# Gated linear attention: the next head's gate inside the first unit, and the backward chunk states on GpSimd beside the forward ones on VectorE

## The reference

```python
def gla_chunked(q, k, v, log_a):            # chunks of C = 64 tokens, N = 16 chunks
    b = jnp.cumsum(gc, axis=-2)             # within a chunk
    ref = b[..., C // 2 - 1:C // 2, :]
    q_in, k_in = qc * jnp.exp(b - ref), kc * jnp.exp(ref - b)
    A = jnp.where(mask, jnp.einsum('nbhid,nbhjd->nbhij', q_in, k_in), 0.0)
    o_intra = jnp.einsum('nbhij,nbhjv->nbhiv', A, vc)
    b_last = b[..., -1:, :]
    q_inter, k_state = qc * jnp.exp(b), kc * jnp.exp(b_last - b)
    decay = jnp.exp(b_last[..., 0, :])
    def step(state, inp):
        qi, ki, vi, di = inp
        o = jnp.einsum('bhid,bhdv->bhiv', qi, state)
        state = state * di[..., None] + jnp.einsum('bhjd,bhjv->bhdv', ki, vi)
        return state, o

def gla_branch(...):
    la_f = jax.nn.log_sigmoid(lr_f @ w_g_f + b_g_f) / GLA_TAU     # and la_b
    o_b = flip(gla_chunked(flip(q), flip(k), flip(v), flip(la_b)))
    o = rmsnorm(o_f + o_b, out_norm)
```

## Time and profile before

| | |
|---|---|
| median of 3 runs | 2673.72 us (2667.28 to 4069.49) |
| the profiled execution | 2673.68 us |
| its span | 2671.9 us |
| busy: TensorE, VectorE, ScalarE, GpSimd | 89%, 48%, 38%, 17% |
| mean granted TensorE clock | 0.949 |

### The profile page before, as it was taken

How to read it: one execution, slowest core, us unless ns; L and a number is a source line. 1 busy time by engine, 2 the same in 40 slices (tenths; PEclk the granted TensorE clock), 3 DMA queues, 4 the chain that set the end, 5 groups by cost and what they waited for, 6 DMA issues and landing times. The chain is left out here.

```text
span 2671.9 us, 31271 instructions
## 1 busy us (share of the span) xinstructions
PE 2373.3 (89%) x11010; PEld 1768.2 (66%) x11010; DVE 1279.2 (48%) x2042; ACT 1023.0 (38%) x1655; POOL 451.1 (17%) x502
## 2 busy tenths in 40 slices
PE   7999677986999994988899997997988899998997
PEld 4877355762444442767677886886776777886885
DVE  4288676323111115455615775354455615775354
ACT  5221366222111114555443444144555543444233
POOL 1058143113222213211111000002211111000000
PEclk9999798897999996999999999998999999999998
DMA  6200300133999887101111003012101110003012
GB/s 193 83 32 1 126 1 1 10 96 112 323 350 341 304 269 281 40 25 32 30 37 28 11 32 127 32 48 94 40 25 32 32 42 20 11 32 127 32 49 86
DMA packets 213549, 239.46 MB, mean 90 GB/s; under 512 B 50849, under 2 KB 170913, under 8 KB 213409
## 3 DMA queue, kind: packets, MB, share of 16 engines
q1 hardware_dynamic: 202928, 220.80, 25.3%
q0 software_dynamic: 9440, 16.83, 1.7%
q10 hardware_dynamic: 1040, 0.00, 0.0%
HBM read 211.80 MB, written 41.52 MB: 95 GB/s over the span
## 5 line engine op out<-in xcount | busy, mean ns | idle before, releaser
L106 PE MATMUL ps<-WT_lo,HT_hi 128*128 128x512 f32 x832 | 327.4, 394 | 0.0
L107 PE MATMUL ps<-HT_hi,WF_lo 128*128 128x512 f32 (+1 forms) x800 | 314.1, 393 | 0.0
L105 PE MATMUL ps<-HT_hi,WU_hi 128*128 128x512 f32 (+1 forms) x704 | 289.5, 411 | 16.6 <-DVE H_lo L2131 13.2
L106 PE MATMUL ps<-H_lo,WU_hi 128*128 128x512 f32 (+1 forms) x704 | 277.4, 394 | 0.0
L1570 PE MATMUL ps<-WT,MIX 128*128 128x512 f32 x496 | 225.0, 597 | 2.9 <-DVE MIX L2089 2.9
L105 PE MATMUL ps<-W_hi,HT_hi 128*128 128x512 f32 x512 | 204.6, 400 | 8.8 <-DVE MIX_lo L2272 5.9
L952 POOL TENSOR_TENSOR WF_lo<-WF,WU_hi 128x1024 fp32r<-128x1024 f32 (+1 forms) x44 | 112.2, 2551 | 567.3 <-ACT WU_hi L1162 567.3
L107 PE MATMUL ps<-W_hi,MIX_lo 128*128 128x512 f32 x512 | 201.8, 394 | 0.0
L106 PEld LDWEIGHTS ps<-WT_lo,HT_hi 128*128 128x128 f32 x832 | 158.9, 191 | 31.9
L107 PEld LDWEIGHTS ps<-HT_hi,WF_lo 128*128 128x128 f32 (+1 forms) x800 | 151.1, 189 | 33.8
L105 PEld LDWEIGHTS ps<-HT_hi,WU_hi 128*128 128x128 f32 (+1 forms) x704 | 133.9, 190 | 56.1 <-DVE H_lo L2131 14.0
(11 more groups left out here) (420 smaller groups left out, 5072.7 us busy)
## 6 DMA issues: line engine op xcount, KB each, us to landing
WT<-in_w_gate SPq DMA_DIRECT2D x31, 1024.0 KB, 5.7
WT<-in_w_up SPq DMA_DIRECT2D x31, 1024.0 KB, 9.2
MIX<-in_w_down SPq DMA_DIRECT2D x31, 1024.0 KB, 8.5
WF<-in_w_in SPq DMA_DIRECT2D x48, 512.0 KB, 3.9
WT<-in_w_out SPq DMA_DIRECT2D x6, 2048.0 KB, 8.1
H<-in_x SPq DMA_DIRECT2D x16, 512.0 KB, 8.1
h_dram<-H SPq DMA_DIRECT2D x16, 512.0 KB, 3.0
H<-h_dram SPq DMA_DIRECT2D x16, 512.0 KB, 11.9
```

Of the source, the lines that this page charges most:

```text
L105: pe.matmul(o, lh, rh, start=(i == 0), stop=False)
L106: pe.matmul(o, lh, rl, start=False, stop=False)
L107: mm = pe.matmul(o, ll, rh, start=False, stop=(i == last))
```

## The change

The gate of head h + 1 is computed earlier. On TensorE `gates(h + 1)` moves between the two halves of head h's first unit and writes banks 6 and 7 (free once `ks_copy(h)` is done), on ScalarE `gate(h + 1)` stands behind the first half's evacuation of that unit, ahead of the second half's, and on VectorE `gate(h + 1)` stands ahead of `scan_states(h)`. The backward states go to GpSimd: `scan_back(h)`, 15 steps of a multiplication and an addition, each waiting for the one before. `gt` = cum - middle goes from VectorE to GpSimd too (`from_middle`). ScalarE's `exps` takes `la` first and then waits for GpSimd's `gt`. `outputs(h)` waits for the backward states as well.

```diff
-            GLA_STEPS[g_pe] += [("a", h), ("kt", h), ("kv", h)] + [("z", h + 1)] * more + [("o", h), ("ms", h)]
+            GLA_STEPS[g_pe] += [("a", h), ("kt", h)] + [("z", h + 1)] * more + [("kv", h), ("o", h), ("ms", h)]
...
+            GLA_STEPS[g_pool] += [("stb", h)] + [("gt", h + 1)] * more
...
-                for u in range(2, 16):
+                def from_middle(h):
+                    pool.wait_ge(*gla(L, "c", h))
+                    settle(pool, settled)
+                    pool.tensor_tensor(gt.rearrange("p (c i) -> p c i", c=NCH), cc, refs.unsqueeze(2).to_broadcast([P, NCH, CH]), ALU.subtract).then_inc(g_pool, 1)
+
+                def scan_back(h):
+                    pool.wait_ge(*gla(L, "kvc", h))
+                    pool.wait_ge(ul_ready, L * NU + 7 + 3 * h)
+                    if h == 0:
+                        settle(pool, settled)
+                        hc.link(pool.memset(st[64:P, NCH - 1, :], 0.0))
+                    for c in range(NCH - 2, -1, -1):
+                        settle(pool, settled)
+                        hc.link(pool.tensor_scalar(st[64:P, c, :], st[64:P, c + 1, :], decay[64:P, c + 1:c + 2], None, ALU.mult))
+                        settle(pool, settled)
+                        o = pool.tensor_tensor(st[64:P, c, :], st[64:P, c, :], kv[64:P, c + 1, :], ALU.add)
+                        if c > 0:
+                            hc.link(o)
+                    o.then_inc(g_pool, 1)
+                    pool.wait_ge(*gla(L, "stb", h))
+                for u in range(2, 5):
                     unit_lo(u)
+                from_middle(0)
+                unit_lo(5)
+                for h in range(4):
+                    unit_lo(6 + 3 * h)
+                    if h < 3:
+                        scan_back(h)
+                        unit_lo(7 + 3 * h)
+                        from_middle(h + 1)
+                        unit_lo(8 + 3 * h)
+                scan_back(3)
...
                 def exps(h):
                     act.wait_ge(*gla(L, "d", h))
+                    act.activation(la, la, ACT.Exp, scale=1 / 16.0)
+                    act.wait_ge(*gla(L, "gt", h))
...
-                    evac(*under[h][0])
+                    evac(*under[h][0], between=(lambda: gate(h + 1)) if h < 3 else None)
                     kv_copy(h)
-                    if h < 3:
-                        gate(h + 1)
                     evac(*under[h][1])
...
-                        mm = pe.matmul(bank(2 + half), wgs[:, h, :], lrz[:, half * HALF:(half + 1) * HALF], start=True, stop=True)
+                        mm = pe.matmul(bank(6 + half), wgs[:, h, :], lrz[:, half * HALF:(half + 1) * HALF], start=True, stop=True)
...
                 def outputs(h):
                     pe.wait_ge(*gla(L, "st", h))
+                    pe.wait_ge(*gla(L, "stb", h))
+                    if h < 3:
+                        pe.wait_ge(*gla(L, "t", h + 1))
...
-                    dve.tensor_tensor(chunks(gt), cc, refs.unsqueeze(2).to_broadcast([P, NCH, CH]), ALU.subtract)
+                    dve.sem_inc(g_dve, 1)
...
-                        dve.scalar_tensor_tensor(out=st[0:64, c, :], in0=st[0:64, c - 1, :], scalar=decay[0:64, c - 1:c], in1=kv[0:64, c - 1, :], op0=ALU.mult, op1=ALU.add)
-                        o = dve.scalar_tensor_tensor(out=st[64:P, b, :], in0=st[64:P, b + 1, :], scalar=decay[64:P, b + 1:b + 2], in1=kv[64:P, b + 1, :], op0=ALU.mult, op1=ALU.add)
+                        o = dve.scalar_tensor_tensor(out=st[0:64, c, :], in0=st[0:64, c - 1, :], scalar=decay[0:64, c - 1:c], in1=kv[0:64, c - 1, :], op0=ALU.mult, op1=ALU.add)
...
                 for h in range(4):
                     causal(h)
+                    if h < 3:
+                        gate(h + 1)
                     scan_states(h)
                     if h < 3:
-                        gate(h + 1)
                         products(h + 1)
                     finish(h)
```

More of the change, by code:

```diff
@@ L397, in program @@
         u_w, u_ready, u_evac = sems("u_w", 2), sem("u_ready"), sems("u_evac", 2)
-        g_pe, g_act, g_dve = sem("g_pe"), sem("g_act"), sem("g_dve")
-        GLA_STEPS = {g_pe: [("z", 0)], g_act: [("t", 0), ("e", 0)], g_dve: [("d", 0), ("k", 0), ("q", 0)]}
+        g_pe, g_act, g_dve, g_pool = sem("g_pe"), sem("g_act"), sem("g_dve"), sem("g_pool")
+        GLA_STEPS = {g_pe: [("z", 0)], g_act: [("t", 0), ("e", 0)], g_dve: [("c", 0), ("d", 0), ("k", 0), ("q", 0)], g_pool: [("gt", 0)]}
         for h in range(4):
             more = h < 3
-            GLA_STEPS[g_pe] += [("a", h), ("kt", h), ("kv", h)] + [("z", h + 1)] * more + [("o", h), ("ms", h)]
-            GLA_STEPS[g_act] += [("ks", h), ("kvc", h)] + [("t", h + 1), ("e", h + 1)] * more + [("sq", h), ("r", h)]
-            GLA_STEPS[g_dve] += [("am", h), ("st", h)] + [("d", h + 1), ("k", h + 1), ("q", h + 1)] * more + [("done", h)]
+            GLA_STEPS[g_pe] += [("a", h), ("kt", h)] + [("z", h + 1)] * more + [("kv", h), ("o", h), ("ms", h)]
+            GLA_STEPS[g_act] += [("ks", h)] + [("t", h + 1)] * more + [("kvc", h)] + [("e", h + 1)] * more + [("sq", h), ("r", h)]
+            GLA_STEPS[g_dve] += [("am", h)] + [("c", h + 1), ("d", h + 1)] * more + [("st", h)] + [("k", h + 1), ("q", h + 1)] * more + [("done", h)]
+            GLA_STEPS[g_pool] += [("stb", h)] + [("gt", h + 1)] * more
         GLA_AT = {step: (s, i) for s, steps in GLA_STEPS.items() for i, step in enumerate(steps)}
@@ L942, in layer @@
             def layer(L):
-                hc = Chain(pool, pool_chain, L * 2 * NT + base)
+                hc = Chain(pool, pool_chain, L * (2 * NT + 117) + base)
                 pool.wait_ge(h_in, L * NT + NT)
@@ L981, in layer @@
                 nt_pool(pool, hc, L * 2 + 4)
-                assert hc.n == 2 * NT
+                assert hc.n == 2 * NT + 117
             layers(pool, layer)
@@ L1220, in gate @@
                         hs, bias = slice(half * HALF, (half + 1) * HALF), vl[:, L_GB + h:L_GB + h + 1]
-                        act.activation(la[:, hs], bank(2 + half), ACT.Identity, bias=bias)
-                        o = act.activation(gt[:, hs], bank(2 + half), ACT.Abs, bias=bias)
+                        act.activation(la[:, hs], bank(6 + half), ACT.Identity, bias=bias)
+                        o = act.activation(gt[:, hs], bank(6 + half), ACT.Abs, bias=bias)
                     hc.link(o)
@@ L1642, in gates @@
                     else:
[L1643 removed]
+                        pe.wait_ge(*gla(L, "ks", h - 1))
                     for half in range(2):
[L1645 removed]
+                        mm = pe.matmul(bank(6 + half), wgs[:, h, :], lrz[:, half * HALF:(half + 1) * HALF], start=True, stop=True)
                     mm.then_inc(g_pe, 1)
@@ L1697, in layer @@
                     inner(h)
-                    unit(*under[h][0])
+                    unit(*under[h][0], between=(lambda: gates(h + 1)) if h < 3 else None)
                     states(h)
-                    if h < 3:
-                        gates(h + 1)
                     unit(*under[h][1])
```

8 lines of the change are left out of this document (3 added, 5 removed).

## The result

The changed kernel takes 2752.5 us (median of 4 runs, 2751.64 the fastest) against 2675.2 us for the kernel before, beside which it ran: 1.0298 times the time, 95% interval 1.0268 to 1.0328. One execution of each kernel was far slower (4069 and 5442 us); the ratio leaves these two out. The forecast was 2760, with slower by over 2% at 0.84. The profiled execution took 2752.74 us, its span 2750.3 us, 79 us more than the profiled one before.

The account below looks back on a forecast made before the run. TensorE, busy 89% of the span, was taken as the bound, with GpSimd's backward scan deciding. Per layer 49.7 - 7.5 + 0.7 + 1.0 = 43.9 us, two layers 88 on 2673.7: 2761, said as 2760; range 2705 to 2800.

Parts of the forecast that it names:

- The waits that go, and TensorE's idle time: TensorE: gates' 6.9 us and squares' 7.6 us a layer go; outputs wait for GpSimd eight times, 13 to 17 us each.
- The copy's end: End of the key-value copy after each head's start, some 3.7 us later in heads 0 to 2, unchanged in head 3.
- The scan: GpSimd's backward scan ends 23.9 us behind the copy in heads 0 to 2, 22.8 in head 3.
- A pair: One multiplication and one addition of GpSimd's backward scan, gaps included: 1.25 us, 15 pairs 18.8 us.
- the gaps: Time between chained GpSimd instructions in the scan: 0.09 to 0.1 us, up to twice that with the settling step.
- rival "worse": Scan with VectorE's hold-up at its upper bound and 0.18 us gaps: 2795, or 2807 with multiplication at 0.70; chance 0.13.
- the lock between the engines: VectorE's forward steps and gate hold up GpSimd's scan: 3.8 us for 15 steps, plus 1.1 in heads 0 to 2.
- The sign that I named: In the profile after, VectorE's forward scan steps would often last longer than 0.34 us.
- The multiplication's price: GpSimd's scan multiplication: 0.61 us by the profile row; the skill page's estimate, 0.4, would make the kernel 25 us faster.
- Outputs and what follows: TensorE's outputs take 8.2 us after a wait, by a lower clock; outputs to next head change by -7.5 us a layer.
- the smaller terms: Per layer: subtraction for gt on GpSimd ahead of head 0, +0.7 us; transposes waiting for the late evacuation, +1.
- The gate's move alone: Without the scan on GpSimd, the earlier gate would be a few us either way; it cannot pay for 50.

Follow-up runs that it names:

- experiment 5: Two runs on the changed kernel: settling step ahead of the backward scan's addition left out, 2748.5 us; GpSimd's scan multiplication written as tensor by tensor, 2721.1 us.
- experiment 1: The kernel before with only the backward scan moved to GpSimd, gate and subtraction for gt left in place: 2754.9 us, ratio 1.0302.
- experiments 3: The changed kernel with both scans back on VectorE, gate's place and subtraction for gt on GpSimd kept: 2696.6 us, ratio 1.0077.
- experiment 4: The kernel before with only the gate's matmuls moved into the first unit, writing banks 6 and 7: 2687.1 us, ratio 1.0051.
- experiment 6: The changed kernel with idle products keeping TensorE busy while it waits for GpSimd's scan: 2743.8 us, ratio 1.0264.
- experiment 8: The kernel before with the gate's matmuls early and VectorE's scans reading key-value products straight from PSUM, without ScalarE's copy: 2647.6 us, ratio 0.9902.
- experiment 7: The changed kernel with GpSimd's backward steps on partitions 0 to 63, as VectorE's, writing a spare buffer, real backward states left zero: 2758.6 us, one run.

## Why the prediction was right

**The waits that go, and TensorE's idle time.** Right. `gates` and `squares` don't wait; the outputs wait for GpSimd eight times, 13.4 to 16.9 us (13 to 17 forecast).

**The copy's end.** +22.9, +23.3, +23.2, +18.9 against +23.2, +23.1, +24.0, +18.9.

**The scan.** The sum was right and two of its terms were not. A pair was put at 1.25 and takes 1.44: multiplication (0.605 for 0.61) and addition (0.451 for 0.46) were right to 0.01 by the rows of other widths, but the gaps were put at 0.09 each from one chained instruction, and are 0.18 and 0.21. The settling step makes 0.10 of the first, as experiment 5 shows. The price of a gap of 0.18 stood in the rival "worse" and belonged in the forecast: +2.9 us a head. Against it, the lock between the engines was put at 4.9 us (heads 0 to 2) and 3.8 (head 3). From the copy's end to the outputs pass 23.7, 24.6, 23.4 and 22.4 us, with 21.7 for 15 undisturbed pairs: all else together is 2.0, 2.9, 1.7 and 0.7. VectorE's forward steps cost a GpSimd instruction 0.05 to 0.11 us, where 0.25 a step had been put. The sign that I named, steps often longer than 0.34 us, came for 34 of 120, by 0.08 to 0.13 us, and nothing waits for them. By the rule of the Trainium skill, "SBUF — State Buffer", "Who interferes with whom", the trace agrees for long instructions: five of GpSimd's in experiment 1 each waited for one of VectorE's to end, and VectorE's steps in experiments 3 and 4 waited for GpSimd's. For the short steps it doesn't as far as whole instructions go: of every 0.40 us they take 0.34, so by the rule each GpSimd instruction of 0.45 or 0.60 would hold up the steps beside it for its whole length, and the most that a step lost was 0.13. The two errors are of the same size and opposite; a forecast that holds its total this way is right in part by luck.

**The multiplication's price.** By the estimate from the Trainium skill's "GPSIMD Engine Reference", "Elementwise — side-by-side cycle accounting", it would have been 0.4; the row said 0.61 and was right for the tensor by scalar form. Experiment 5 has 0.397 for the tensor by tensor form, in which the same product can be written.

**Outputs and what follows.** The outputs were taken at 8.2 us and took 7.4, 6.8, 7.8 and 7.5; the cause given (the clock) is shown by experiments 4 and 6. From the outputs to the next head pass 21.8, 19.6 and 20.7 us (22.3, 20.7, 21.0 forecast). Against before that is -3.6, +0.1 and -5.9, with 0.7 less in head 3: -10.1 for my -7.5.

**The sum.** 48.4 - 10.1 = 38.3 a layer, 77 in all, of the 79 between the two profiled executions; my 88 was 9 too high. The outputs and what follows gave 2.6 a layer less than put, 5 of the 9, and the smaller terms of 0.7 and 1.0 a layer don't show: head 0 starts at 1131.80 (1131.99 before), and the transposes' waits (4.2 us in heads 0 to 2) lie ahead of copies that end about as forecast.

**Where it was wrong.** "The gate's move alone" was called a few us either way. With both scans on VectorE the gate's move and the subtraction on GpSimd cost 23 us (2696.6 against 2673.6). The working missed that VectorE's gate then stands between the copy and 30 steps, not 15, and that GpSimd's subtraction and low part then hold up two of these steps. In the changed kernel it is nothing, as the first experiment shows. The parts don't add up: scan alone +81, the rest alone +23, both +77. The prediction also took head 3's wait of 4.27 us for the plain length of the scan; 2.0 us of it are one step held up by GpSimd.

## What to carry to other kernels

A chain of small instructions goes to another engine at that engine's price for each link, gaps included: 11.6 us on VectorE for both scans became 15 x 1.446 = 21.7 for one. Two engines that hold each other up do so both ways: look for a short instruction of the one that lasts as long as a long one of the other, here 2.4 us for 0.34. Before a wait is removed, look at what stands next on the same chain: here a wait ahead of the outputs or ahead of the next head took over, grew together out of several short ones, and cost the clock as well. What helped was to shorten the chain itself, by reading from PSUM what had been copied out of it, which also ended the holding up.

## What the runs showed that I had not expected

- GpSimd, 64x128: tensor by scalar (a pointer per partition) 0.605 us, tensor by tensor with the column repeated 0.397, addition 0.451.
- A chained instruction on GpSimd starts 0.08 us after the one before has ended where it waits itself, 0.18 with a settling step ahead.
- VectorE's 64x128 step costs the same with one input in PSUM (353 ns) as with it in SBUF (352).
- A VectorE step of 0.34 us with both tensor inputs in SBUF lasts 2.3 to 2.5 us where it meets GpSimd's low part of 2.4 (8 of 8 heads in experiment 4); with one of them in PSUM it meets the low part as often and stays at 0.34 to 0.36 (experiment 8).
- VectorE and GpSimd on different halves of the partitions hold each other up as on the same half: experiment 7, one run.
- TensorE's clock after short waits isn't settled by their length alone: outputs ran at 1.00 after 2.60 us and at a mean of 0.76 after 2.14 (experiment 6).
